# Down products inside the next pass of a streamed mixture of experts, on one core

## What is computed

```python
expert = grp[:, None] * EXPERTS_PER_GROUP + local        # two experts per token
h = jax.nn.silu(xblk @ w_gate[e]) * (xblk @ w_up[e])     # 1024 -> 512
return h @ w_down[e]                                     # 512 -> 1024
...
y = jnp.zeros((t, d), yb.dtype).at[buf_tok].add(yb * buf_gate[:, None], mode='drop')
x = layer_norm(ALPHA * x + moe_out, ln2_g[l], ln2_b[l])
```

## Time and profile before

| | |
|---|---|
| median of 3 runs | 1109.23 us (1108.68 to 1109.91) |
| profiled execution, whole | 1111.02 us |
| its span | 1109.3 us |
| TensorE busy | 993.4 us (90%) |
| VectorE, ScalarE, GpSimd busy | 469.6, 279.3, 219.2 us |
| pass 0's first matmul | 628.9 us |
| DMA queue of weights, whole span | 240.54 MB |
| granted TensorE clock, mean | 0.972 of full |

### The profile page before, as it was taken

One profiled execution on the slowest core, in us unless ns is written; L12 is line 12 of the kernel. 1 busy time (PEld: TensorE's weight loads), 2 busy tenths in 40 slices (PEclk: granted clock), 3 DMA queues, 4 the chain that ended last, 5 costly groups with the idle time before them and its releaser, 6 DMA issues.

```text
span 1109.3 us, 16552 instructions
## 1 busy us (share of the span) xinstructions
PE 993.4 (90%) x6068; PEld 464.9 (42%) x6069; DVE 469.6 (42%) x1006; ACT 279.3 (25%) x461; POOL 219.2 (20%) x331
## 2 busy tenths in 40 slices
PE   7999999999999999999994588889888888888774
PEld 3644465466457447444454233333333333332221
DVE  0695542563373363422336134433344444442333
ACT  1123312321322232200001023333333333332331
POOL 3000010010010010033000123333333333343332
PEclk9999999999999999999995599999999999999998
DMA  9332211210220220473709599999999999999992
GB/s 274 121 78 73 58 40 40 71 44 21 76 55 24 57 58 2 154 271 136 320 35 399 167 400 415 397 411 416 417 416 415 415 416 416 415 415 415 419 397 87
DMA packets 93855, 256.68 MB, mean 231 GB/s; under 512 B 15444, under 2 KB 60500, under 8 KB 68976
## 3 DMA queue, kind: packets, MB, share of 16 engines
q1 hardware_dynamic: 81904, 240.54, 56.3%
q0 software_dynamic: 11104, 13.29, 3.4%
q10 hardware_dynamic: 800, 2.15, 0.5%
HBM read 260.90 MB, written 21.23 MB: 254 GB/s over the span
## 4 chain that ended last, share of the span: by engine, by line
PE 52%; DMA 14%; SPq 12%; DVE 8%; issue 8%; POOL 4%; ACT 1%; POOLq 1%; DVEq 0%; ACTq 0%
PE proj L1282 11%; SPq L461 11%; PE proj L1241 11%; DMA y_rows<-const,raw 8%; PE proj L1462 5%; PE bank L1372 5%; PE bank L1450 5%; PE bank L1533 3%; DMA xT_sb<-w_gu 3%; DMA out<-raw 2%; PE bank L1554 1%; PE proj L1249 1%; POOL pass_sb L528 1%; POOL const L544 1%; PE proj L1260 1%
## 5 line engine op out<-in xcount | busy, mean ns | idle before, releaser
L1282 PE MATMUL proj<-xT_sb,ring 128*128 128x512 f32 x384 | 182.1, 607 | 0.0
L1533 PE MATMUL bank<-arena 128*64 128x512 f32 x544 | 122.1, 596 | 16.2 <-PE bank L1554 9.5
L1167 DVE TENSOR_TENSOR raw<-bank,const 128x512 f32<-128x512 f32 x33 | 22.8, 691 | 242.4 <-DMA out<-raw 242.3
L1241 PE MATMUL proj<-xT_sb,ring 128*128 128x512 f32 (+1 forms) x272 | 119.1, 594 | 0.0
L1282 PEld LDWEIGHTS proj<-xT_sb,ring 128*128 128x128 f32 x384 | 68.3, 189 | 68.3 <-issue 64.8
L1533 PEld LDWEIGHTS bank<-arena 128*64 128x64 f32 x544 | 43.0, 137 | 95.1 <-issue 82.8
L1241 PEld LDWEIGHTS proj<-xT_sb,ring 128*128 128x128 f32 (+1 forms) x272 | 50.7, 188 | 64.6 <-issue 64.5
L1533 PE MATMUL bank<-gates,arena 128*64 128x512 f32 x256 | 60.2, 622 | 8.4 <-PE bank L1554 4.8
L752 ACT ACTIVATE pass_sb<-bank 128x256 f32<-128x256 f32 x33 | 12.7, 383 | 201.1 <-PE bank L1533 201.1
L1372 PEld LDWEIGHTS bank<-arena 64*64 64x64 f32 x1536 | 52.8, 134 | 18.2 <-ACT arena L703 9.1
L499 POOL MEMSET arena<- 64x64 f32 x8 | 1.2, 145 | 291.7 <-DVE arena L923 257.9
(11 more groups left out here) (278 smaller groups left out, 1349.6 us busy)
## 6 DMA issues: line engine op xcount, KB each, us to landing
arena<-w_gu SPq DMA_DIRECT2D x64, 1024.0 KB, 22.4
gates<-w_gu SPq DMA_DIRECT2D x32, 1024.0 KB, 20.8
arena<-w_down SPq DMA_DIRECT2D x24, 1024.0 KB, 23.1
ring<-w_in SPq DMA_DIRECT2D x42, 512.0 KB, 3.9
gates<-w_down SPq DMA_DIRECT2D x16, 1024.0 KB, 22.7
branches<-w_down SPq DMA_DIRECT2D x16, 1024.0 KB, 25.6
xT_sb<-w_gu SPq DMA_DIRECT2D x16, 1024.0 KB, 24.9
ring<-w_gu SPq DMA_DIRECT2D x16, 1024.0 KB, 24.4
```

Source lines behind the costliest of these rows:

```text
L1241: ins = pe.matmul(proj[0:w, b, :], ring[:, slot, k, 0:w], xT_sb[:, k, :], start=(k == 0), stop=(k == KT - 1))
L1282: ins = pe.matmul(proj[:, gate_at["bank"], :], ring[:, gate_at["slot"], k, :], xT_sb[:, k, :], start=(k == 0), stop=(k == KT - 1))
L1533: ins = pe.matmul(bank[SLOTS * h:SLOTS * h + SLOTS, 0, :], xeT[:, k % 4, SLOTS * (k // 4):SLOTS * (k // 4) + SLOTS], gu[k // 2][:, k % 2, ...
```

## The change

TensorE: the down products of a pass leave `one_pass` and become `down`, called in the next pass between its second and third k tile (and once at the end). `pair_stats` comes before the seventh k tile. `one_pass` is written once in `expert`, followed by the loop for further passes. The first four experts are unrolled. Each pass, not only an expert's last, counts `s_used` up six times; SyncE works out from the routing tables, loaded to registers, which count an expert's last pass reaches, and waits for that. The order of reloads is now: chunks 1, 2, 3 of expert e, chunk 0 of expert e + 1, chunks 4, 5 of expert e. VectorE's `normed` joins `finish` of the same pass, ScalarE's square root follows the pass's own `y_e`, GpSimd issues `scatter_out(p)` before it waits for `y_low` and issues `lower_rows(p + 1)`. Up to two further passes are written out on ScalarE and VectorE instead of looped.

```diff
-            def reload(e, b, used):
-                for c in range(NCH):
-                    sp.wait_ge(s_used, used + c + 2)
...
+            def uses_through(e):
+                extra = sp.value_load(extra_i[0:1, bass.ds(e, 1)], min_val=0, max_val=MORE)
+                first = sp.value_load(first_i[0:1, bass.ds(e, 1)], min_val=0, max_val=PASSES - 2)
+                return (first + extra) * USES
+            def reload_expert(e, b, last=False):
+                used = uses_through(e - SETS)
+                for c in (1, 2, 3):
+                    reload(e, b, c, used + (c + 3))
+                if not last:
+                    reload(e + 1, (b + 1) % SETS, 0, uses_through(e + (1 - SETS)) + 1)
+                for c in (4, 5):
+                    reload(e, b, c, used + (c + 4))
...
                 next_tokens(p + 1)
                 scatter_lower(p)
+                scatter_out(p, first)
                 pool.wait_ge(s_ylow, p * 16 + 16)
-                pool.wait_ge(s_base, p + 2)
                 lower_rows(p + 1)
-                scatter_out(p, first)
...
+            def one_pass(p, b, loads, before):
                 pe.wait_ge(s_xeT, p + 1)
                 gu = [v.rearrange("p (k h n) -> p k h n", k=2, h=2) for v in w_chunk[b][0:4]]
                 for k in range(KT):
+                    if k == 2 and before:
+                        down(*before)
+                    if k == 6:
+                        pair_stats(p)
...
+                        if k == 2 and h == 0:
+                            ins.then_inc(s_used, 1 if before else 2)
                     if k == KT - 1:
                         ins.then_inc(s_hp, 1)
-                    elif k % 2 == 1 and last:
+                    elif k % 2 == 1:
                         ins.then_inc(s_used, 1)
                 turn(p + 1)
-                pair_stats(p)
                 pe.wait_ge(s_h, p + 1)
...
-                if last:
-                    pe.sem_inc(s_used, 1)
+                pe.sem_inc(s_used, 1)
...
-                    products(p)
-                    normed(p - 1)
-                    finish(p, n)
+                    products(p)
+                    finish(p, n)
...
                 act.wait_ge(s_yp, p + 2)
                 act.activation(y_e, bank[:, 1, :], ACT.Copy, scale=gate_tab[:, bass.ds(p, 1)]).then_inc(s_ye, 1)
+                act.activation(warm[:, 2:3], warm[:, 0:1], ACT.Sqrt)
+                act.wait_ge(s_dev, p + 1)
+                act.activation(half_rs[:, 2:3], pair[:, 1:2], ACT.Sqrt, bias=half_rs[:, 1:2], scale=0.5).then_inc(s_root, 1)
```

More of the change, by code:

```diff
@@ L775, in _ @@
             more = act.value_load(more_i[0:1, 0:1], min_val=0, max_val=MORE)
-            with act.If(more > 0):
-                with act.Fori(0, more) as i:
+            for n in range(2):
+                with act.If(more > n):
+                    one_pass(N_EXP + n, n)
+            with act.If(more > 2):
+                with act.Fori(2, more) as i:
                     one_pass(i + N_EXP, None)
-            deviation(more + (N_EXP - 1))
         @block.vector
@@ L1208, in _ @@
                     products(p)
-                    normed(p - 1)
                     finish(p, n)
             more = dve.value_load(more_i[0:1, 0:1], min_val=0, max_val=MORE)
-            with dve.If(more > 0):
-                with dve.Fori(0, more) as i:
+            for n in range(2):
+                with dve.If(more > n):
+                    products(N_EXP + n)
+                    finish(N_EXP + n, n)
+            with dve.If(more > 2):
+                with dve.Fori(2, more) as i:
                     products(i + N_EXP)
-                    normed(i + (N_EXP - 1))
                     finish(i + N_EXP, 0)
-            normed(more + (N_EXP - 1))
         @block.tensor
@@ L1523, in pair_stats, with down @@
                 ins.then_inc(s_pair, 1)
[L1525 to L1546 removed]
+            def down(p, b, loads):
                 pe.wait_ge(s_hT, p + 1)
@@ L1562, in _, with expert @@
             pe.sem_inc(s_yp, 1)
-            def expert(e, b, loads):
+            def expert(e, b, loads, first_of_all=False):
                 extra = pe.value_load(extra_i[0:1, bass.ds(e, 1)], min_val=0, max_val=MORE)
                 first = pe.value_load(first_i[0:1, bass.ds(e, 1)], min_val=0, max_val=PASSES - 2)
-                pe.wait_ge(s_yp, first + 1)
-                pe.sem_inc(s_used, 1)
+                one_pass(first, b, loads, () if first_of_all else (first - 1, (b - 1) % SETS, loads if b else loads - 16))
                 with pe.If(extra > 0):
                     with pe.Fori(0, extra) as n:
-                        one_pass(first + n, b, loads, False)
-                one_pass(first + extra, b, loads, True)
-            with pe.Fori(0, N_EXP // SETS) as i:
+                        one_pass(first + n + 1, b, loads, (first + n, b, loads))
+            for b in range(SETS):
+                expert(b, b, 16, first_of_all=b == 0)
+            with pe.Fori(1, N_EXP // SETS) as i:
                 for b in range(SETS):
@@ L1578, in _ @@
             more = pe.value_load(more_i[0:1, 0:1], min_val=0, max_val=MORE)
+            down(more + (N_EXP - 1), SETS - 1, 16 * (N_EXP // SETS))
             pair_stats(more + N_EXP)
```

63 lines of the change are left out of this document (29 added, 34 removed).

## The result

The changed kernel takes 1150.95 us (median of 4 runs, 1149.92 to 1152.95) against 1109.07 us in runs beside it: ratio 1.0379, interval 1.0361 to 1.0397. That is slower, as forecast, but by 41.9 us, twelve times the forecast 3.4 us. The profiled run took 1151.16 us as a whole, its span is 1149.1 (before 1109.3). Up to base add 1 the forecast holds: 662.18, forecast 661.6. All of the loss is in the stage and its tail.

A forecast was written before the change was run, and what follows sets the result against it. Before, transfers and a chain of 33 passes run side by side, weights pacing the end. GpSimd's loop at 14.32 us a pass instead of 13.67 moves the last sum from 1099.51 to 1102.9: +3.4, 1112.6 us, range 1106.5 to 1118.5.

The forecast's parts named there:

- TensorE's loop: TensorE's pass through ScalarE in the new order: 13.1 to 13.6 us, fitting inside GpSimd's loop.
- the register loads: TensorE ahead of k0: two loads with their branch, at most 0.7 us a pass if not hidden.
- GpSimd's loop: Queue order closes a loop from lower_rows through base add, norm and scatter_out: 14.32 us a pass against 13.67, deciding the time.
- The clock: TensorE's clock in the expert stage: taken at full, with no term for it in the sum.
- The ScalarE leg and its table loads: ScalarE between square root and silu: 1.28 us load, 0.20 us activation, delaying silu 0.4 us; no further drain.
- SyncE's gap: SyncE at expert 5: stops at 28 chunks, about 696 us; transfers end 3 to 5 us later; costed at nothing.
- Unrolling and counting: Counting uses in each pass and unrolling the first four experts: nothing but code, -0.5 to +1 us.
- The tail: End of the stage: base add 31 at 1091.2, last sum through TensorE at 1102.9.
- C: Rival, 0.17: loop 14.5 us or more through longer landings, a missed slot at k6 or table loads; 1118 at 14.5.
- A: Rival, 0.16: GpSimd's loop 14.0 us or less, transfers stay the bound, tail gets shorter: -2.4 us, 1106.8.
- B: Rival, 0.17: loop 14.2 us or less, but the transfer gap at expert 5 decides: +1.3 us, 1110.5.
- the turning point: Pace where the forecast's side turns: 14.2 us a pass; base add 31 is 3.6 us earlier, the sum -0.2.

The follow-up runs named there:

- e13: Changed kernel with the end of a pass (turn, wait for h, transposes) moved behind the next expert's register loads, loop kept: 1118.23 us, ratio 1.0077.
- e8: Kernel before with two unused register loads between a pass's transposes and its down products: 1114.04 us, ratio 1.0047.
- e3: Changed kernel with TensorE's two register loads done twice for each expert, the second pair unused: 1204.61 us, ratio 1.0851.
- e4: Changed kernel with 13 small unused matmuls in TensorE's two idle places of each pass, register loads left bare: 1138.64 us, ratio 1.0257.
- e10: Kernel before with only GpSimd's new order, down left in its old place: 1155.51 us, ratio 1.0427.
- e9: Changed kernel with SyncE issuing chunks 4 and 5 before the wait for the next expert's chunk 0 (old order): 1152.82 us, ratio 1.0386.
- e16: e15 with SyncE's old order of chunks: 1112.85 us, ratio 1.0039.
- e18: e15 with small filler matmuls in TensorE's two waits and SyncE's old order of chunks: 1114.86 us, ratio 1.0053.
- e1: Changed kernel with TensorE's loop over experts written out for all 32, register loads left where they are: 1148.9 us, ratio 1.0359.
- e15: e13 with GpSimd copying the index of lower_rows before scatter_out: 1110.54 us, ratio 1.0017.
- e12: e2 with 3 filler matmuls before the wait for h, 10 ahead of the statistics, and the old order of chunks: 1157.12 us, ratio 1.0441.
- e2: e1 with the next expert's register loads moved between turn and the wait for h: 1134.48 us, ratio 1.0218.
- e11: e2 with one more, unused bn_stats (0.69 us) on VectorE ahead of the statistics: 1147.65 us, ratio 1.0348.

## Why the prediction was wrong, point by point

The direction was right, the size was not: 1150.95 against a range that ended at 1118.5. In the span the miss is 1149.1 - 1112.7 = 36.4 us. Base add 31 came at 1121.24 instead of 1091.2, 30.0 us; from there to the last sum it took 18.1 us instead of 11.7, 6.4 us.

The direction was right also for the forecast's own reason: with the loads hidden and its loop in place, e13 is 9.2 us slower than before. But three quarters of the loss, 32.7 of 41.9 us, are not that loop.

**The step that failed is TensorE's loop, in the term of the register loads.** I took them from the idle time ahead of k0 in the kernel before, 0.7 us, and made the loop 13.1 to 13.6. That 0.67 us is not theirs at all. The loads ran under down, and the sequencer was done with them 2.2 us before down ended; the 0.67 us is the wait for down's own end and the branch behind it (L1568, L1569), and e8 leaves it at 0.67 with two more loads ahead of down. The change puts the loads behind two short transposes, with nothing queued to cover them: 1.5 us for the two with their arithmetic and 0.3 to the start of k0, a gap of 1.8 (50.6 us in the waits). Measured from 867.35 to 882.26, TensorE's pass is 14.91 at full clock; without the 1.94 of the gap and the 0.26 ahead of the statistics it is 12.7, so the other terms of that sum were, taken together, if anything too long. (The sum itself was not added up right: its terms give 13.15 with the table's 0.4 inside the 1.5, or 13.55 with it on top, and with the 0.7 of the loads 13.85 or 14.25, not 13.6. Each is still under the 14.32 of GpSimd's loop, so the forecast did not turn on it.) I had the right sentence in the text (those loads "if not hidden") and the wrong price beside it. e13 shows it directly: loads hidden, 32.7 us gone. e3 shows it the other way.

**The clock was not in the sum at all.** I had it at full, as it was in the stage before. Two idle places in a pass of 15 us, 0.8 and 1.9 us, and the granted clock falls to 1.2 GHz for 3 us in every second pass, which makes that pass 1.3 to 1.6 us longer. e4 restores the clock with the loads bare: 12.3 us. A page of the Trainium skill, TensorE: Matmul & The Clock Gate, section "A second HAM failure mode: psum-queue depth-cycling", describes such a thing for a kernel that cycles through its PSUM banks: short idle times between groups of matmuls make the clock swing between its two levels. The trace agrees in kind: 1.94 and 3.57 us for eight records each, in turn, and full clock once the idle places are filled (e4). Here what leaves the engine idle is the wait for h and the register loads. Why it is every second pass is open: ahead of the fast pair the engine had stood 0.81 and 1.94 us, ahead of the slow one 0.83 and 2.10.

**The ScalarE leg and its table loads** were right by the trace; in the pass shown above the silu starts 0.47 us behind the last k tile, forecast 0.4. In after:

```profile
879.63 0.26 ACT L777 ACTIVATE half_rs<-bank,half_rs 128x1 f32<-128x1 f32 x1 [2.20 <-DVE half_rs L1194]
879.91 1.28 ACT L763 ACT_TABLE_LOAD   x1
881.21 0.20 ACT L763 ACTIVATE raw<-raw 128x1 f32<-128x1 f32 x1
```

The load follows the square root within 0.02 us and the activation follows the load within 0.02 us. The further drain of 1.38 us of the Trainium skill, ScalarE: Activation LUTs, section "What ACT_TABLE_LOAD costs", is seen neither ahead of the load nor behind it; on the page of the profile, the idle time ahead of all 66 loads is 2.0 us together.

**GpSimd's loop** was right in its mechanism: base adds are released by the y_low gather, and e10 shows that the queue order alone makes a loop of this kind. In size: forecast 14.32; in after itself its legs are stretched to 15.32 by TensorE (the sum waits for y_e, 1.14 instead of 0.83, the norm steps take 3.55 instead of 3.29, and `lower_rows` waits for the landing of a later `scatter_lower`, 2.47 instead of 2.09); with TensorE out of the way they are 14.34 (e13). As the statement of what decides, "this is the part that I think decides", it was wrong: it was the second bound, not the first. e13's 1118.23 is what the whole change would have given if only the forecast's loop had counted; the 5.6 us above my 1112.6 I put down mostly to GpSimd's delay in pass 27 (2.7 us) and to the passes around expert 5 (15.8 and 16.6 us); that was not tried apart.

**SyncE's gap** was right in place and count: 28 chunks, then a stop. It began at 700.2, later than my 696, and lasted until 717.5, 5 us later than forecast because the passes are longer. Costed at nothing, and it costs nothing (e9, e16, e18).

**Unrolling and counting** at -0.5 to +1: e1 goes further in the same direction and moves the time by -2 us, within its interval.

**The tail** was forecast at 11.7 us from base add 31 to the last sum. In after:

```profile
1121.24 0.69 DVE L1181 TENSOR_TENSOR raw<-bank,const 128x512 f32<-128x512 f32 x1 [4.17 <-DMA const<-y_rows,raw]
...
1127.06 0.26 PE L1534 MATMUL bank<-arena,const 128*64 128x2 f32 x4
...
1133.08 5.35 PE L1546 MATMUL bank<-branches,pass_sb 128*64 128x512 f32 x16 [1.43 <-DVE pass_sb L1170]
...
1139.34 0.69 DVE L1184 TENSOR_TENSOR raw<-raw,const 128x512 f32<-128x512 f32 x1 [3.57 <-ACT const L774]
```

The statistics of pass 31 are 5.8 us behind the base add and not 2.4, since y_e is late (TensorE again): 3.4 of the 6.4 us. The last down ran partly at half clock, 5.35 us instead of 3.65: 1.7. The rest, 1.3, lies between the statistics and down, 6.0 us instead of 4.6.

**The rivals.** C (loop of 14.5 or more) had the direction, but its reasons were landings, a missed slot at k6 and table loads; none of these did it. A and B needed a loop under 14.2 us, which was reached only in e15 to e18, with loads hidden and the index copied early. The price that I gave for the turning point (14.2) fits e15: 14.0 us and 0.17% above before, although not the gain that A gave for it, since transfers and the long pass take it back.

## What to carry to other kernels

Ask of each instruction of the sequencer (register load, branch) not how much idle time stands near it now but which queued work it runs under, and read who ended the idle time; when a change moves it behind a wait and short operations, price it at its own full length, here 0.3 us for the load alone and 0.6 to 0.8 with its arithmetic. Then add up the new idle places of TensorE in a pass: where they grow, take the half clock into the sum. And when an engine's in-order queue closes a loop through other engines, sum that loop, but also sum every other engine's loop with its overheads bare, since the longest decides.

## What the runs showed of the hardware

- TensorE's sequencer runs ahead of the array: two loads with arithmetic from 874.7 to 876.1 under a down that lasts to 878.3, at no cost that is seen; the same two bare cost 1.23 us more each pass (e3), and 0.5 where a wait for a copy covers part (e8).
- The granted clock in the stage: 0.95 in after, 1.00 with thirteen small matmuls in each pass's idle places (e4), 0.98 with the gap ahead of k0 gone (e13), 0.90 with gaps of 3 us (e3, half clock in nearly every pass). Filler ahead of an operation in the critical loop costs its overshoot: 0.75 us a pass in e12.
- Two indirect DMAs in a row on GpSimd start 2.05 us apart with an index copy between them and 1.30 us apart without (e15).
- A load of ScalarE's tables took 1.28 us in all; the next activation started 0.02 us behind it or sooner, and the idle time ahead of the 66 loads of after is 2.0 us together.
- The landing of the y_low gather goes with the code beside it: 6.5 to 6.8 us from issue to base add in the looped kernels, 7.0 to 7.2 in the ones written out (e1, e2, e11, e12), whose instruction queue moves 64 to 77 packets instead of 37 to 44. That one causes the other is an inference.
- GpSimd stands 2.7 us in pass 27 with no wait that is seen, in each kernel with its new order and in the kernel before in its own way; the cause is open.
